# Memory keys moved to the first seam, zero matmuls at the lead-in, finer waits, in a two-block fp32 transformer kernel

## What is computed

```python
# first block
y = jnp.concatenate([y_a, y_b], axis=-1).astype(hn.dtype)
mix = jnp.matmul(y, w_out)
x = x + rms_norm(mix, norm_mix_post[l])
hn = rms_norm(x, norm_ffn_pre[l])
ff = conv_ffn(hn, ...)
# second block, layer l
x = x + pool_conv_mixer(rmsnorm(x, norm_mix_g[l]), ...)
m = rmsnorm(mem, norm_mem_g[l])            # mem: 256 x 1024, independent of x
k, v = jnp.split(m @ wkv, 2, axis=-1)
s = jnp.einsum("bthd,bmhd->bhtm", q, k) * (XA_HEAD_DIM ** -0.5)
```

## Time and profile before

| what | value |
|---|---|
| median of 3 runs | 2017.86 us (2017.0 to 2018.45) |
| the profiled execution: its own time, its span | 2019.5 us, 2017.7 us |
| PE busy | 1993.6 us, 99% of the span |
| DVE, ACT, POOL busy | 47%, 31%, 72% |
| chain that ended last | PE 98% |
| mean granted TensorE clock | 0.997 |
| DMA | 190.79 MB, mean 95 GB/s |

### The profile page before, as it was taken

The page is one execution under the profiler, slowest core; times in us unless marked ns, Lnnn a source line. Parts: engine busy times, 40 slices in busy tenths (PEclk is TensorE's granted clock), DMA queues, the critical chain, the costliest instruction groups (busy, mean ns, idle before and its releaser), DMA issues.

```text
span 2017.7 us, 25748 instructions
## 1 busy us (share of the span) xinstructions
PE 1993.6 (99%) x9490; PEld 1629.8 (81%) x9490; DVE 954.0 (47%) x1578; ACT 616.6 (31%) x1172; POOL 1448.2 (72%) x736
## 2 busy tenths in 40 slices
PE   8999989999999999999999999999999999999998
PEld 6787778888888888788888888877678888888887
DVE  4566544233433898465431332363655653223134
ACT  5454442221013434433210110235743321111012
POOL 7623379777777877874977778687569388787774
PEclk9999999999999999999999999999999999999999
DMA  4741233332323345321333323233013123232322
GB/s 164 145 66 63 74 110 105 95 103 94 95 90 108 105 146 168 105 84 42 115 94 95 103 85 105 74 104 113 11 32 105 53 87 104 94 102 94 101 85 66
DMA packets 58298, 190.79 MB, mean 95 GB/s; under 512 B 6416, under 2 KB 10256, under 8 KB 58096
## 3 DMA queue, kind: packets, MB, share of 16 engines
q1 hardware_dynamic: 54720, 184.42, 30.1%
q10 hardware_dynamic: 3472, 4.88, 0.8%
HBM read 183.50 MB, written 2.10 MB: 92 GB/s over the span
## 4 chain that ended last, share of the span: by engine, by line
PE 98%; DVE 1%; ACT 1%; DMA 0%; POOL 0%; issue 0%; SPq 0%; DVEq 0%; ACTq 0%
PE bank L744 30%; PE bank L746 30%; PE bank L745 30%; PE bank L1465 2%; PE bank L1122 1%; PE bank L1479 1%; PE bank L1495 1%; PE bank L1033 1%; PE bank L804 0%; PE bank L1195 0%; PE bank L1144 0%; DMA raw<-weights 0%; PE bank L977 0%; PE bank L1364 0%; PE bank L1139 0%; PE bank L1278 0%
## 5 line engine op out<-in xcount | busy, mean ns | idle before, releaser
L631 POOL TENSOR_TENSOR wH<-raw,zero 128x1024 fp32r<-128x1024 f32 (+1 forms) x303 | 579.5, 1913 | 389.0 <-PE bank L746 371.8
L634 POOL TENSOR_TENSOR wL<-raw,wH 128x1024 fp32r<-128x1024 f32 (+1 forms) x303 | 719.5, 2375 | 23.8
L744 PE MATMUL bank<-hnH,wH 128*128 128x512 f32 (+1 forms) x1456 | 575.6, 395 | 13.8 <-POOL wL L625 7.4
L745 PE MATMUL bank<-hnL,wH 128*128 128x512 f32 (+1 forms) x1456 | 569.2, 391 | 0.0
L746 PE MATMUL bank<-hnH,wL 128*128 128x512 f32 (+1 forms) x1456 | 569.1, 391 | 0.0
L744 PEld LDWEIGHTS bank<-hnH,wH 128*128 128x128 f32 (+1 forms) x1456 | 274.0, 188 | 77.9 <-DVE hnL L2254 15.5
L746 PEld LDWEIGHTS bank<-hnH,wL 128*128 128x128 f32 (+1 forms) x1456 | 274.0, 188 | 58.8 <-issue 0.9
L745 PEld LDWEIGHTS bank<-hnL,wH 128*128 128x128 f32 (+1 forms) x1456 | 274.2, 188 | 58.5 <-issue 2.1
L744 PE MATMUL bank<-actH,wH 128*128 128x512 f32 (+1 forms) x802 | 309.8, 386 | 0.0
L746 PE MATMUL bank<-actH,wL 128*128 128x512 f32 (+1 forms) x802 | 308.3, 384 | 0.0
L745 PE MATMUL bank<-actL,wH 128*128 128x512 f32 (+1 forms) x770 | 295.7, 384 | 0.0
(11 more groups left out here) (415 smaller groups left out, 2575.1 us busy)
## 6 DMA issues: line engine op xcount, KB each, us to landing
raw<-weights SPq DMA_DIRECT2D x315, 512.0 KB, 3.5
raw<-weights SPq DMA_DIRECT2D x28, 384.0 KB, 3.0
XT<-x_t SPq DMA_DIRECT2D x8, 256.0 KB, 6.2
XT<-x_t ACTq DMA_DIRECT2D x1, 2048.0 KB, 8.3
maxB<-rowM SPq DMA_DIRECT2D x7, 256.0 KB, 14.6
out<-MIX SPq DMA_DIRECT2D x13, 128.0 KB, 1.8
qkO<-qkA SPq DMA_DIRECT2D x4, 256.0 KB, 4.1
memT<-mem_t ACTq DMA_DIRECT2D x1, 1024.0 KB, 5.4
```

Of the source, the lines that this page charges most:

```text
L631: nc.gpsimd.tensor_tensor(wH[:, slot, 0:w], raw[:, slot, 0:w], nothing.broadcast_to([P, w]), ALU.add)\
L634: nc.gpsimd.tensor_tensor(wL[:, slot, 0:w], raw[:, slot, 0:w], wH[:, slot, 0:w].bitcast(F32), ALU.subtract).then_inc(split, 1)
L744: mm(out_, aH, bH, start=first, stop=False)
L745: mm(out_, aH, bL, start=False, stop=False)
```

## The change

- **Order of units and tiles.** `mem_k0` 0 and 1 move to between `w_out` and `ff0_gu0`; PE does them after `post_sums("post0")`. The other key tiles move up: 2 before `post_sums("post1")`, 3 to 5 after it, 6 and 7 after `pc_in`. Units 0, 1, 6, 7 leave the list `MEMORY`, so POOL makes both of their halves.
- **Memory.** `memT` is loaded before `XT` comes back. ACT and DVE square and sum it into `rmem` ahead of the `w_out` copies. The PE sum `mem_sums` stands after `w_out` tile 3. The root and the halves are made between `post_chunk` 2 and 3, from PSUM banks 3 and 4. The same work leaves `ff0_d0` and `ff0_d1`.
- **Post norm 0.** Its table load goes (the set is the one in use). ACT copies the first key tile to `KTA`, and later from there to `KT[0]`.
- **Lead-in.** Four fp32 matmuls of zeros (16 columns by 512) before the first chunk and one after the second chunk; `a_qk` tile 0 lags three chunks instead of two, and tile 1 comes after the loop.
- **Waits.** `gone_wait` of `P1` and `P2` moves to just ahead of the matmuls that read them; DVE's `actL` stands ahead of the gate scaling; at the end `scale(5)` stands ahead of `sum_half(1, 6)`.

```diff
     elif _n == "pc_in":
-        SEQ += [("mem_k0", _i) for _i in range(4)]
+        SEQ += [("mem_k0", _i) for _i in range(2, 6)]
...
+    elif _n == "w_out":
+        SEQ += [(_n, _i) for _i in range(_c)] + [("mem_k0", _i) for _i in range(2)]
...
-MEMORY += [POS["mem_k0", _i] for _i in range(8)]
+MEMORY += [POS["mem_k0", _i] for _i in range(2, 6)]
...
-TILES += [("w_out", (0, 1, 2)), ("norm_b", (2, 3)), ("w_out", range(3, 8)), ("post0", 1)]
+TILES += [("w_out", (0, 1, 2)), ("norm_b", (2, 3)), ("w_out", (3,)), ("mem_sums", 1), ("w_out", range(4, 8)),
+          ("mem_k0a", (0,)), ("post0", 1)]
...
+            def keep_busy(times, n):
+                for _ in range(times):
+                    mm(psum(n)[0:16, :], zero[:, 0:16], zero[:, 0:1].broadcast_to([P, S]), start=True, stop=True)
+            pe.wait_ge(sig("zero_set"), 1)
+            keep_busy(4, TILE0["cum"])
             for k in range(KD):
                 wait_hn("mix_pre", k)
                 lead_in(k)
-                if k >= 2:
-                    key_query(0, k - 2)
-                if k >= 5:
-                    key_query(1, k - 5)
-            key_query(0, 6)
-            key_query(0, 7)
+                if k == 1:
+                    keep_busy(1, TILE0["cum"])
+                if k >= 3:
+                    key_query(0, k - 3)
+            for k in range(KD - 3, KD):
+                key_query(0, k)
+            for k in range(3):
+                key_query(1, k)
             first_sums()
...
                     gone_wait(pe, TILE0[f"lev{cc}_7"] + hh)
-                    gone_wait(pe, TILE0[f"lev{cc}_8"] + hh)
-                    gone_wait(pe, TILE0[f"lev{cc}_9"] + 2 * hh)
-                    gone_wait(pe, TILE0[f"lev{cc}_9"] + 2 * hh + 1)
...
+                    gone_wait(pe, TILE0[f"lev{cc}_8"] + hh)
...
-            project("w_out", actH, actL, ready=mixed_ready, lead=3)
+
+            def memory_sums():
+
+                n = TILE0["mem_sums"]
+                pe.wait_ge(sig("mem_added"), KD)
+                claim(n)
+                mm(psum(n)[:, 0:MEM], ones, rmem[:, :], start=True, stop=True).then_inc(tile_done, 1)
+            project("w_out", actH, actL, ready=mixed_ready, lead=3, after={3: memory_sums})
...
             post_sums("post0")
+            memory_key(0)
+            memory_key(1)
             feed_forward(0, "ffn_pre")
-            memory_key(0)
+            memory_key(2)
             post_sums("post1")
-            for i in (1, 2, 3):
+            for i in (3, 4, 5):
                 memory_key(i)
...
-            for i in range(4, 8):
+            for i in (6, 7):
                 memory_key(i)
...
-                nc.scalar.preload_act_table_set("natural_log_exp_and_others")
+                if post == "post1":
+                    nc.scalar.preload_act_table_set("natural_log_exp_and_others")
...
+            def memory_halves():
+
+                n = TILE0["mem_sums"]
+                tile_wait(act, n)
+                link(run(psum(n)[:, 0:MEM], psum(n)[:, 0:MEM], ACT.Ln, bias=v("eps"), scale=1.0 / D))
+                run(psum(n)[:, 0:MEM], psum(n)[:, 0:MEM], ACT.Exp, scale=-0.5).then_inc(sig("mem_root"), 1)
+                for c_ in range(KD):
+                    act.wait_ge(sig("mem_normed"), c_ + 1)
+                    high(memH[0][:, c_, :], memory_bank(c_), v("mem0", c_))
+                    run(memT[:, c_, :], memory_bank(c_), ACT.Copy).then_inc(sig("mem_kept"), 1)
             for m in range(KD):
+                if m == 3:
+                    memory_halves()
...
+            run(KT[0][:, 0:2, :], KTA[:, :, :], ACT.Copy)
...
+                def half_low(c_):
+                    dve.wait_ge(sig("mem_kept"), c_ + 1)
+                    low(memL[0][:, c_, :], memory_bank(c_), v("mem0", c_), memH[0][:, c_, :])
+                    dve.wait_ge(hn_ready, nhn[0])
...
+                scale(5)
                 sum_half(1, KD - 2)
-                scale(5)
                 add_half(1, KD - 1)
...
-                    if lev % 2 and lev > 1:
-                        scaled((gateO, gateR)[cc][:, h, :], TILE0[("a_o", "b_r")[cc]] + h)
```

More of the change, by code:

```diff
@@ L195 @@
         TILES += [(f"ff{_i}_gu{_t}", 2 * _c)]
-        if (_i, _t) == (0, 0):
-            TILES += [("ff0_d0", range(4)), ("mem_sums", 1), ("ff0_d0", range(4, 8))]
-        else:
-            TILES += [(f"ff{_i}_d{_t}", 8 if (_i, _t) != (2, 2) else WHOLE)]
+        TILES += [(f"ff{_i}_d{_t}", 8 if (_i, _t) != (2, 2) else WHOLE)]
 TILES += [("end0", 3), ("end1", (0,)), ("row_sum_end", (0,)), ("end1", (1, 2)), ("row_sum_end", (1,))]
@@ L389, in program @@
         rmem = at("rmem", [P, MEM], offset=up2)
+        KTA = at("KTA", [P, 2, MEM], offset=up2 + 7680)
+        assert up2 + 7680 + KB2 <= TOP
         sinT = at("sinT", [P, NB, 32], offset=up2 + 1088)
@@ L880, in feed_forward @@
                     project(f"ff{f}_d{t}", actH, actL, kd=chunks, lead=2,
-                            after={3: lambda: row_sums(TILE0["mem_sums"], "mem", MEM)} if (f, t) == (0, 0) else {},
                             ready=lambda k: gone_wait(pe, TILE0[f"ff{f}_gu{t}"] + 2 * k + 1))
@@ L1617, in feed_forward @@
                     if t == 0 and f == 0:
-                        act.wait_ge(mem_in, 48)
-                        for c_ in range(KD):
-                            square(memT[:, c_, :], MEM)
+                        act.wait_ge(mem_in, 32)
                         for m in range(KD):
@@ L1849, in _ @@
             head_high(3)
+            act.wait_ge(sig("mem_raw"), 16)
+            for c_ in range(KD):
+                if c_ < 2:
+                    gone_wait(act, TILE0["norm_b"] + 2 + c_)
+                else:
+                    act.wait_ge(sig("mem_added"), c_ - 1)
+                run(memory_bank(c_), memT[:, c_, :], ACT.Square).then_inc(sig("mem_sq"), 1)
             def post_chunk(n, m):
@@ L1880, in post_norm @@
                         new_square(c_ - 1)
+                if first == 0:
+                    tile_wait(act, key_tile(0))
+                    free(run(KTA[:, :, :], psum(key_tile(0))[:, :].rearrange("p (t m) -> p t m", t=2), ACT.Copy),
+                         key_tile(0))
                 for c_ in range(0 if first == 0 else KD - 1, KD):
@@ L1949, in _ @@
                     memory_input(1)
-            for i in range(4, 8):
-                memory_high(GATES + i)
             for i in range(28):
-                if i < 4:
+                if i in (2, 3):
                     memory_key(0, 4 + i)
@@ L2283, in convolve, with memory_squares @@
                 stt(acc, pad[:, right:right + S], v(w, 3 * q + 2), acc, ALU.mult, ALU.add).then_inc(sig("conv_done"), 1)
-            def memory_norm():
-                dve.wait_ge(mem_in, 48)
-                for c_ in range(KD):
-                    add_squares(c_ == 0, MEM)
-                dve.wait_ge(sig("mem_root"), 1)
-                for c_ in range(KD):
-                    tt(memT[:, c_, :], memT[:, c_, :], rmem[:, :], ALU.mult).then_inc(sig("mem_normed"), 1)
+            def memory_squares():
+                for c_ in range(KD):
+                    dve.wait_ge(sig("mem_sq"), c_ + 1)
+                    if c_ == 0:
+                        last = nc.vector.tensor_copy(rmem[:, :], memory_bank(c_))
+                    else:
+                        dve.wait_ge(sig("mem_added"), c_)
+                        last = tt(rmem[:, :], memory_bank(c_), rmem[:, :], ALU.add)
+                    last.then_inc(sig("mem_added"), 1)
+            def memory_norm():
+                n = TILE0["mem_sums"]
+                dve.wait_ge(sig("mem_root"), 1)
+                def half_low(c_):
+                    dve.wait_ge(sig("mem_kept"), c_ + 1)
+                    low(memL[0][:, c_, :], memory_bank(c_), v("mem0", c_), memH[0][:, c_, :])
+                    dve.wait_ge(hn_ready, nhn[0])
+                for c_ in range(KD):
+                    tt(memory_bank(c_), memT[:, c_, :], psum(n)[:, 0:MEM], ALU.mult).then_inc(sig("mem_normed"), 1)
+                    if c_ > 0:
+                        half_low(c_ - 1)
+                dve.wait_ge(sig("mem_normed"), KD)
+                half_low(KD - 1)
+                free(nc.vector.tensor_copy(tmpY[:, :], psum(n)[:, 0:1]), n)
             def memory_low(l, c_):
```

53 lines of the change are left out of this document (29 added, 24 removed).

## The result

The changed kernel takes 2022.07 us (median of 13 runs, 2021.52 to 2023.27); the kernel before took 2018.22 in the 13 runs beside it. The ratio is 1.0021, 95% interval 1.0013 to 1.0028: slower by 3.85 us. The forecast was 2018.9 in a range from 2009.7 to 2022.0; the measured time lies 0.07 us above the upper end. The profiled execution has a span of 2020.5 us, 2.8 more than that of before, and an own time of 2022.25, 0.2 above its median.

What follows compares the result with a forecast made beforehand. PE was taken as the bound, busy 1993.6 of 2017.7 us. The terms -2.6 - 1.9 + 3.9 - 0.4 - 0.5 - 0.4 = -1.9 us became +1.0 with one clock fall: 2017.86 + 1.0 = 2018.9 us, range 2009.7 to 2022.0.

Steps and rivals of the forecast that it cites:

- Lead-in: Start of the kernel: zeros raise the clock early, so the first sums start at 22.6 instead of 25.22; 2.6 us gained.
- gated attention: Gated attention: PE's waits at the turns go through finer waits and an earlier actL; 1.9 us gained, bounds 0.5 and 1.9.
- mem_sums: The memory sum leaves ff0_d0 for w_out, where a wait hides it; 0.4 us gained.
- end: End of the kernel: scale(5) goes into a wait of 0.46 us, so the add comes earlier; 0.4 us gained.
- Memory chain at nothing: Memory root between post_chunk 2 and 3: done by 265, covered by 5 us of slack, so costed at nothing.
- First seam: Between w_out and ff0_gu0: POOL's queue makes PE wait 5 us for chunk 1 despite the key tiles; 3.9 us lost.
- Rival A: First seam: POOL is not late, so -2.4 us instead of +3.9; 2009.7 us in all; chance 14%.
- Mixer: Where the two key tiles left: PE waits about 5 us behind DVE's taps, so 0.5 of 5.76 us is kept.
- Rival B: Mixer: the cover is not needed because DVE's chain starts earlier; -5.3 us, 2010.7 to 2013.6; chance 8%.
- the one on the clock: Seam and mixer gaps: about 5 us, just past the 4.8 before a clock fall; one fall (35%) gives 2018.9 us.
- rival C: Seam and mixer: both gaps halve the clock, 2.9 us each, and a bound slips; 2021.8 us; chance 20%.
- The price of 2.9: Seam and mixer: each fall of the clock to half costs 2.9 us, taken from the seam of the kernel before.

Runs made afterwards that it cites:

- e11: The changed kernel without the five matmuls of zeros at its start, the rest of the lead-in's order kept; 2021.67 us.
- e1: The changed kernel with POOL's steps for the odd chunks of hnL ahead of the split of ff0_gu0 unit 3 instead of behind it; 2029.08 us.
- e9: e1 with the running sum of the squares behind post norm 0 kept in PSUM bank 0 instead of SBUF; 2016.79 us.
- e3: The changed kernel with five fp32 matmuls of zeros in each of its two gaps, seam and mixer; 2020.40 us.
- e2: The changed kernel with ACT's value copies ahead of its wait for the convolutions and PE's pool_group(0) one unit later; 2020.71 us.
- e6: e2 with PE's pool groups 0 to 3 moved later and ACT's pool_take to match; 2020.40 us.
- e4: The kernel before with only the lead-in, the finer waits and actL of the gated attention, and scale(5); no key or memory work moved; 2013.93 us.
- e5: e1 with the row sums of ff0_gu0 behind tile 5 instead of tile 3; 2016.42 us.
- e8: The changed kernel with the edits of e5 and e6 together; 2015.45 us.
- e12: e3 with three matmuls of zeros in each gap instead of five, all at its start; 2020.53 us.

## Why the prediction was wrong

**Lead-in, gated attention, `mem_sums`, end.** Right in size: -2.3, -1.7, -0.5 and -0.4 in the table, for -2.6, -1.5, -0.4 and -0.4. For the first the cause given, that the zeros raise the clock, is not what earned it: `e11` has the sums at 22.82 without them. That it came out right is luck so far.

**Memory chain at nothing.** Right: done at 258.5, its estimate was 265, and DVE's steps with one SBUF input stayed at 0.48 us beside POOL, as the prediction expected.

**First seam.** The wait was right in mechanism and size. POOL's odd chunk was to start "near 286" and started at 286.31, behind ten unbroken units; PE waited 1.2 and 4.5. `e1` and `e9` show the cause by taking it away. Rival A is out. But the seam had a bound that the prediction put at nothing: the adds of squares for the sums, slow beside POOL. In the changed kernel it stays hidden behind the late queue and the half clock; as soon as either goes, PE waits for it (10.0 us in `e1`, 1.4 in `e3`).

**Mixer.** Right too: 4.7 us at the claim of bank 2, behind `cvb` and the taps, for "about 5". Rival B is out. `e2` and `e6` add that the bound was not that wait alone: with it gone DVE's chain and ACT's order put most of the same time one or two steps on.

**The step that failed** is the one on the clock: "Before, the clock fell at about 282.3, 4.8 us after the last matmul", so two gaps of about 5 us were "just past that, so neither is sure", and one fall, not two, was made the likeliest, 2018.9. That made a fixed delay out of a single row. The runs show none. These are all the gaps of 2.5 us or more between PE's matmuls in the traces, with the stretch at half clock that came in or just behind each, and the longest gaps without one:

| kernel, place | gap, us | clock falls, us after PE stopped | half clock, us | of it with PE at work |
|---|---|---|---|---|
| before, seam | 5.6 | 4.6 | 6.8 | 5.9 |
| changed, seam | 4.5 | 2.0 | 6.8 | 4.3 |
| changed, mixer | 4.7 | 3.6 | 6.8 | 5.7 |
| `e1`, sums | 10.0 | 2.3 | 13.7 | 6.0 |
| `e1`, mixer | 4.7 | 3.6 | 6.8 | 5.7 |
| `e2`, seam | 4.5 | 0.9 | 6.8 | 3.2 |
| `e2`, mixer | 2.6 | 3.6 | 3.4 | 3.4 |
| `e4`, seam | 5.6 | 2.5 | 6.8 | 3.8 |
| `e5`, mixer | 4.7 | 5.0 | 3.4 | 3.4 |
| `e6`, seam | 4.5 | 2.4 | 6.8 | 4.7 |
| `e6`, mixer | 3.5 | 4.1 | 3.4 | 3.4 |
| `e8`, mixer | 3.5 | 2.7 | 6.8 | 6.0 |
| `e9`, mixer | 4.7 | 4.9 | 3.4 | 3.4 |
| `e11`, seam | 4.5 | 0.8 | 6.8 | 3.1 |
| `e11`, mixer | 4.7 | 2.9 | 6.8 | 5.0 |
| `e12`, both | 1.8, 2.05 | no fall | 0 | 0 |

Every gap from 2.6 us up was followed by half clock, none of 2.05 or less was, and the fall came between 0.8 and 5.0 us after the last matmul. The earliest falls are in the seam, in `e2` and `e11`, behind a wait of 1.2 us that PE had a microsecond before. In `e2` PE stops at 283.35 (windows, PE alone):

```profile
283.25:284.00 0.75, 0.10 (x1) 1.00 0.54 109
284.00:284.50 0.50, 0.00 (x0) 0.73 0.85 295
```

With two falls the steps give +3.9, 2021.8, the case called rival C, which had 20%. The changed kernel is that case: both windows show 0.50. The price of 2.9 was near the upper end. Half of the time that PE works at half clock is 2.2 and 2.8 here, and 1.5 to 3.0 over the gaps of the table, since what falls into the gap itself is free. The Trainium skill (TensorE: Matmul & The Clock Gate, Why this matters for your kernels) warned that idle gaps between bursts bring the half clock back. Taken as a rule without exception it made two falls the likeliest case, as the prediction said. On the gaps of this table from 2.6 us up it holds, and on the two short ones of `e12` it doesn't.

**Luck in the 3.9.** The measured +3.85 looks like rival C to a twentieth of a microsecond, but two errors cancel in it. In the traces the change adds 2.8, not 3.9: 0.8 less for the two half clocks and 0.4 less from the other steps together. And the step from the profiled execution to the medians was wrong by 1.1 the other way: the profile of before stood 1.3 us above its median, that of the changed kernel 0.2. The prediction had taken the full 1.6 off and so counted on the same lateness in both. Of the miss of 3.2 us, 1.7 is in the trace, where the second half clock is the largest term, and 1.5 is the choice of the starting point (0.4 of it is that 3 runs of before gave 2017.86 and 13 gave 2018.22).

**What the clock is worth.** The case without a fall was forecast at 2016.0. `e3` has no fall and takes 2020.40. So two more terms were too small: the sums' wait for the adds of squares, put at nothing, is 1.4 us there, and the starting point is about 1.5 again. The rest is mostly 0.5 in the lead-in and about 1 in the mixer and the convolution.

**Chances and range.** The chance of "slower by over 4.0" is given as 0.13; its parts, half of C and the 5%, add up to 0.15. The upper end of the range, 2022.0, was rival C with 0.2 us to spare, though that case alone had 20%.

## What to carry to other kernels

Moving work out of a stage to fill a gap elsewhere needs three answers: which engine prepares its operands and what stands behind it in that queue (here two weight units put 8.6 us of splitting ahead of four normalisation steps), what the work was covering where it stood, and what in-order copy frees the next bank there. When a wait is removed, list the next bound before counting the gain: here DVE's adds beside POOL made PE wait 10 us where 4.5 were won. A gap of some microseconds costs at most its length plus half of the half-clock stretch that reaches into the work behind it. A few matmuls of zeros in a gap that must stay kept the clock up, but they gave back 1.7 us of 5.0 here, because another bound stood close behind. And where a forecast goes from one profiled execution to a median, the place of that execution among the runs is an error of its own, here over 1 us.
